# w_up on x before its norm, gains put on by ScalarE, x updated in 1024-wide steps, two more streams begun with pairs of tiles

## The chip, the cores and the metric

One core of a Trainium2 chip. The metric is the device time of one execution in microseconds (us). All times below are us from the start of the profiled span unless marked otherwise.

## The reference, cut to what matters

A state-space and attention block of two layers, then a second block (RWKV and latent attention, a feed-forward net with a causal convolution, and a gated embedding), for 256 tokens of width 2048. All of it is float32. The change lies in the last part of the second block:

```python
h = h + rms_norm_2(mix, post_mix_norm)          # mix = (...) @ w_out
u = rms_norm_2(h, pre_ffn_norm)
up = causal_dwconv(u @ w_up, conv_w, conv_b)    # per channel, over 3 tokens
gate, val = jnp.split(up, 2, axis=-1)
f = (jax.nn.gelu(gate, approximate=True) * val) @ w_down
h = h + rms_norm_2(f, post_ffn_norm)
e = p @ w_ple
h = h + rms_norm_2(jax.nn.sigmoid(h @ w_ple_gate) * e, ple_norm)
```

where `rms_norm_2(x, g) = x * rsqrt(mean(x * x) + 1e-6) * g`, the mean over the 2048 channels of a token. The token's factor is one number per token, so it can be put on before or after the product with w_up.

## The kernel before

Activations lie transposed: x is 16 tiles (k) of 128 channels (partitions) by 256 tokens, side by side in one region, 4096 columns wide. A norm's factor is a number per column (token), held in RS as a 128x256 tile; a gain is a number per partition. So the mean over channels is a sum over tiles (VectorE or TensorE) and over partitions (a TensorE product with ones).

**Products.** Each weight matrix is a *stream* of output tiles n, each the sum over k of blocks of 128x128 weights with 128x256 activations. Both operands are split into a rounded high part (`hi`, a ScalarE copy) and a low part (`lo`, VectorE: value minus high part), and a block is three matmuls of 256 columns: high x high, high x low, low x high. The third waits for the weight's low part. Weights come by DMA in units of 1 MB (16 blocks) into a ring of three places; a unit is split in two *halves* of 8 blocks (1024 columns). A half p has one ScalarE `hi` and one VectorE `lo`, in one of four buffers: `hi` p waits until TensorE has done half p-4. For the activations the same pair of instructions is run for each k (256 wide).

**Order.** One Python class, `Timeline`, plays the schedule once and writes a list of beats; each engine's program goes through this list and emits its part of each beat, so the order on every engine is that of the list, and ScalarE and VectorE wait in order. `stream` (L428) emits, at the start of half p, `hi` of half p+3 and `lo` of half p+2, then the matmuls, and after every half one phase of each tile that is finished but not yet evicted (`leave`, L400; `follow`). The number of phases per kind of tile is in `PHASES` (L238); which phase frees the accumulator bank is in `BANK_FREE`. At a stream's end all phases left over are run at once (`while self.pend: self.follow()`). Streams named in `PAIRS` (L276) begin with their first two tiles interleaved: k 0 to 7 of tile 0, k 0 to 7 of tile 1, k 8 to 15 of tile 0, k 8 to 15 of tile 1. `late` is work put in after block 39 of a stream, with the finished tiles held until then; w_in2 uses both.

**The streams here.** w_out2 (16 tiles of 16 blocks, kind "mo"), w_up (44 tiles), w_down0 (16 tiles of 22 blocks), w_up (44 tiles more), w_ple (16 tiles of 2 blocks), w_down1 (16 of 22), w_pg (16 of 16).
- Eviction of "mo": ScalarE copies 0.5 x the sum to MO, squares it, VectorE adds the square to RS2. Those of "d1" (w_down1) and "pg" (w_pg) end in the same square and addition.
- `rms` (L992, L1325): TensorE product with ones, ScalarE square root; `recip`: VectorE reciprocal into RS.
- `post` (L2049), 16 times: VectorE scales a tile by gain and RS, then adds it to x. It is run after w_out2, after w_down1 and after w_pg (where SyncE writes out every fourth).
- After w_out2: sixteen ScalarE squares of x (`sq`), 16 TensorE products with ones in their wake, a second root and reciprocal; then `h` (L1728) for each k: VectorE product of x, gain and RS, ScalarE high part, VectorE low part. Only then w_up begins. After w_down1, high and low parts of x (`part "xs"`) are made k by k.
- Eviction of w_up, alternately "up0" (gate) and "up1" (value), a pair j makes one hidden tile: ScalarE multiplies the accumulator by the third tap and adds the bias, VectorE adds the two other taps reading the accumulator (255 and 254 columns); up0 goes on with a polynomial (VectorE, three instructions), tanh (ScalarE), a product (VectorE); up1 multiplies by it, and the hidden tile's high part (ScalarE) and low part (VectorE) follow. The phases are one half apart.

L822 is tensor_tensor, L832 scalar_tensor_tensor, L840 reciprocal, L859 activation, L862 matmul: helpers through which every such instruction is recorded.

## Time and profile before

| | us |
|---|---|
| median of three runs (lowest, highest) | 3351.78 (3350.07, 3360.97) |
| the profiled execution | 3350.08 |
| its span | 3348.3 |
| TensorE busy | 3019.5 (90%) |
| VectorE busy | 2286.7 (68%) |
| ScalarE busy | 1623.7 (48%) |
| GpSimd busy | 316.1 (9%) |
| the chain that ended last: TensorE, VectorE, ScalarE, DMA | 63%, 23%, 6%, 5% |

PE is TensorE, PEld its weight loads, DVE VectorE, ACT ScalarE, POOL GpSimd. PEclk is the granted TensorE clock as a share of full speed (2.4 GHz at 1.0, 1.2 GHz at 0.5). A row of a timeline gives the start, the time from the first start to the last end of xN like instructions in a row, and in brackets the idle time before them with what ended it.

### The profile page before, as it was taken

The page shows a single profiled execution, that of the slowest core. Times are in us where ns is not written, and L with a number is a line of the kernel's source. Part 1 is how long each engine was busy: PE and PEld are TensorE (multiplying, and loading weights), DVE is VectorE, ACT ScalarE, POOL GpSimd, SP SyncE. Part 2 cuts the span into 40 slices and gives each one's busy share as a digit, 9 for nine tenths or more (in the row PEclk, how much of TensorE's full clock was granted, in tenths as well). Part 3 has the DMA queues.
Part 4 walks back from the last instruction along what each step waited for, and adds up shares of the span by engine and source line. Part 5 has one row for each costly group of instructions (what it writes and reads, how often), then busy time and mean ns, then how long its engine had stood idle before and what let it go on. Part 6 is the DMA issues. An engine that isn't in the chain of part 4 may idle for free.

```text
span 3348.3 us, 59688 instructions
## 1 busy us (share of the span) xinstructions
PE 3019.5 (90%) x24116; PEld 2777.9 (83%) x24116; DVE 2286.7 (68%) x3591; ACT 1623.7 (48%) x2408; POOL 316.1 (9%) x566
## 2 busy tenths in 40 slices
PE   6799898889998998999899898799899999999977
PEld 1577777768888888998878788789799999999977
DVE  6467776677688867775666666666688745886565
ACT  3345554345465644744444442544455544555443
POOL 0012222100122220200000001010000000000000
PEclk8899999889999998999999998899899999999988
DMA  9776656665644454454323222345355555554533
GB/s 386 282 241 214 221 209 235 239 227 179 166 141 133 148 165 160 167 190 145 107 94 106 96 104 84 135 140 195 114 169 187 183 184 181 184 188 168 181 132 114
DMA packets 110707, 576.92 MB, mean 172 GB/s; under 512 B 33056, under 2 KB 33088, under 8 KB 46688
## 3 DMA queue, kind: packets, MB, share of 16 engines
q1 hardware_dynamic: 89040, 525.37, 45.0%
q0 software_dynamic: 20816, 44.27, 4.6%
q8 instruction: 190, 3.11, 0.4%
q10 hardware_dynamic: 576, 3.47, 0.3%
q14 instruction: 85, 0.70, 0.1%
HBM read 546.83 MB, written 17.83 MB: 169 GB/s over the span
## 4 chain that ended last, share of the span: by engine, by line
PE 63%; DVE 23%; ACT 6%; DMA 5%; issue 3%; SPq 1%; POOL 1%; DVEq 0%; ACTq 0%; POOLq 0%
PE acc L862 62%; DVE arena L822 6%; DVE rounded L822 5%; DVE arena L832 3%; DVE upper L822 3%; DMA arena<-in_w_ada 2%; ACT arena L859 2%; ACT rounded L859 2%; DMA arena<-in_w_in 1%; DVE upper L832 1%; ACT upper L859 1%; DVE upper L840 1%; PE acc L865 1%; SPq L818 1%; ACT L859 1%
## 5 line engine op out<-in xcount | busy, mean ns | idle before, releaser
L862 PE MATMUL acc<-rounded 128*128 128x256 f32 x14832 | 1962.2, 292 | 64.9 <-issue 47.2
L862 PEld LDWEIGHTS acc<-rounded 128*128 128x128 f32 x14832 | 1867.3, 196 | 152.2 <-issue 117.6
L822 DVE TENSOR_TENSOR rounded<-arena,rounded 128x1024 fp32r<-128x1024 f32 (+1 forms) x860 | 1013.7, 1179 | 377.8 <-ACT rounded L859 310.2
L859 ACT ACTIVATE rounded<-arena 128x1024 fp32r<-128x1024 f32 (+1 forms) x876 | 884.4, 1010 | 654.7 <-PE acc L862 501.4
L862 PEld LDWEIGHTS acc<-upper_rounded,rounded 128*128 128x128 f32 x4416 | 546.2, 197 | 40.7 <-DVE rounded L822 21.5
L862 PE MATMUL acc<-upper_rounded,rounded 128*128 128x256 f32 x4416 | 553.6, 288 | 19.3 <-DVE rounded L822 19.2
L862 PE MATMUL acc<-arena 128*32 128x512 f32 (+7 forms) x1898 | 276.0, 465 | 98.3 <-DMA arena<-in_w_ada 43.8
L859 ACT ACTIVATE arena<-arena 128x256 f32<-128x256 f32 (+3 forms) x377 | 191.3, 507 | 237.5 <-DVE arena L822 153.7
L822 DVE TENSOR_TENSOR arena<-arena 128x256 f32<-128x256 f32 (+5 forms) x543 | 264.1, 486 | 40.5 <-ACT arena L859 17.1
L862 PEld LDWEIGHTS acc<-arena 128*32 128x32 f32 (+4 forms) x1898 | 127.2, 141 | 166.8 <-DMA arena<-in_w_ada 65.9
L859 ACT ACTIVATE arena<-acc 128x256 f32<-128x256 f32 (+4 forms) x300 | 125.1, 417 | 254.1 <-PE acc L862 237.1
L862 PE MATMUL acc<-upper 128*128 128x128 f32 (+9 forms) x1632 | 195.1, 298 | 14.8 <-DVE upper L822 10.2
L859 ACT ACTIVATE arena<-acc,arena 128x256 f32<-128x256 f32 (+1 forms) x210 | 100.8, 480 | 183.2 <-PE acc L862 175.7
L862 PEld LDWEIGHTS acc<-upper 128*128 128x128 f32 (+4 forms) x1632 | 155.0, 168 | 40.3 <-DVE upper L822 13.3
L822 DVE TENSOR_TENSOR arena<-acc,arena 128x256 f32<-128x256 f32 (+2 forms) x192 | 81.6, 425 | 152.7 <-PE acc L862 141.8
L832 DVE SCALAR_TENSOR_TENSOR arena<-acc,arena 128x255 f32<-128x255 f32 (+2 forms) x244 | 118.6, 486 | 84.7 <-ACT arena L859 40.2
L832 DVE SCALAR_TENSOR_TENSOR arena<-arena 128x256 f32<-128x256 f32 (+5 forms) x349 | 151.4, 434 | 32.5 <-ACT arena L859 14.1
L818 POOL DMA_DIRECT2D arena<-arena x256 | 130.5, 517 | 423.4 <-ACT arena L859 416.7
L859 ACT ACTIVATE upper<-acc 128x256 f32<-128x256 f32 (+4 forms) x176 | 88.2, 501 | 159.6 <-PE acc L862 112.4
L862 PE MATMUL acc<-upper,arena 64*64 64x64 f32 (+3 forms) x546 | 89.4, 364 | 42.8 <-DVE upper L822 26.4
L862 PEld LDWEIGHTS acc<-upper,arena 128*128 128x128 f32 (+2 forms) x546 | 57.4, 174 | 60.8 <-DVE upper L822 29.8
L865 PE MATMUL acc<-arena 128*128 128x128 f32 x384 | 72.1, 282 | 28.3 <-ACT arena L859 23.0
(88 smaller groups left out, 1170.7 us busy)
## 6 DMA issues: line engine op xcount, KB each, us to landing
arena<-in_w_in SPq DMA_DIRECT2D x164, 1024.0 KB, 5.0
arena<-in_w_ada SPq DMA_DIRECT2D x88, 1024.0 KB, 5.4
arena<-in_w_up SPq DMA_DIRECT2D x88, 1024.0 KB, 4.8
arena<-in_w_down SPq DMA_DIRECT2D x44, 1024.0 KB, 4.9
arena<-in_w_outa SPq DMA_DIRECT2D x16, 1024.0 KB, 7.0
arena<-in_w_glu SPq DMA_DIRECT2D x16, 1024.0 KB, 5.3
arena<-in_w_outm SPq DMA_DIRECT2D x16, 1024.0 KB, 5.0
arena<-in_w_out SPq DMA_DIRECT2D x16, 1024.0 KB, 4.8
```

What stands on the lines that cost most here:

```text
L818: self.e.dma_start(out, in_).then_inc(self.signals.sems[sem], 16)
L822: return self.put(self.e and self.e.tensor_tensor(o, a, b, op))
L832: return self.put(self.e and self.e.scalar_tensor_tensor(out=o, in0=a, scalar=s, in1=b, op0=o1, op1=o2))
L840: return self.put(self.e and self.e.reciprocal(o, a))
L859: return self.put(self.e and self.e.activation(o, a, f, scale=scale, **kw))
L862: return self.put(self.e and self.e.matmul(o, l, r, start=start, stop=stop, skip_group_check=True))
L865: return self.put(self.e and self.e.transpose(o, i, self.m.con("ident")))
```

## The change

- `post` handles four tiles at once: VectorE multiplies 4x256 by RS (repeated), then adds 1024 columns to x. The gains are put on by ScalarE: for w_out2 in the eviction copy (scale 0.5 x post_mix, made once in w_in2's time), for w_down1 and w_pg by an extra copy in place after the square.
- "mo" is squared from the accumulator, ahead of its copy.
- After w_out2 and its reciprocal, `post` of a group alternates with `hf` (high part by ScalarE with the gain as scale, low part by scalar_tensor_tensor on VectorE) and `sqf` (ScalarE squares 1024 columns, GpSimd adds them up). w_up thus runs on x times gain, without the token factor. Its root and reciprocal are `late` in w_up (after block 39), and each w_up tile gets a first phase in which VectorE multiplies the accumulator by RS into a scratch slot; the other phases read that slot.
- After w_down1, high and low parts of x are made 1024 wide (`xs`), each after its `post`.
- w_up and w_pg are in `PAIRS`; `ready` asks for their first units ahead of `recip`.
- `stream` lets held tiles go one at a time.

```diff
-"mo": 3, "up0": 3, "up1": 4
+"mo": 2, "up0": 4, "up1": 5          # PHASES; BANK_FREE of up0, up1: "ev_dve" -> "ev_rs"
...
-PAIRS = (("w_in", 48), ("w_in2", 0))
+PAIRS = (("w_in", 48), ("w_in2", 0), ("w_up", 0), ("w_pg", 0))
...
-            if late is None or blk == 39:
-                if late is not None:
-                    late()
-                    late = None
-                for t in held:
-                    g = self.leave(t)
-                    next(g)
-                    self.pend.append((t, g))
-                held = []
+            if late is not None and blk == 39:
+                late()
+                late = None
+            if held and late is None and (k == nk - 1 or blk % 8 == 7):
+                t = held.pop(0)
+                g = self.leave(t)
+                next(g)
+                self.pend.append((t, g))
...
         self.rms("mo", ("w_out2", 0, 15))
+        self.ready("w_up", 0)
         self.add("recip", "mo")
-        for k in range(16):
-            self.add("post", "mo", k)
-        for k in range(16):
-            self.add("sq", "hf", k)
-        self.rms("hf", None)
-        self.add("recip", "hf")
-        for k in range(16):
-            self.add("h", 3, k)
+        for g in range(5):
+            if g < 4:
+                self.add("post", "mo", g)
+            if g:
+                for k in range(4 * g - 4, 4 * g):
+                    self.add("hf", k)
+                self.add("sqf", g - 1)
         self.add("ff_first")
-        self.stream("w_up", 0, 0, 0, 44, 16)
+
+        def late():
+            self.add("rmsf")
+            self.add("recip", "hf")
+
+        self.stream("w_up", 0, 0, 0, 44, 16, late=late)
...
         self.rms("fo", ("w_down1", 0, 15))
+        self.ready("w_pg", 0)
         self.add("recip", "fo")
-        for k in range(16):
-            self.add("post", "fo", k)
-        for k in range(16):
-            self.add("part", "xs", k)
+        for g in range(5):
+            if g < 4:
+                self.add("post", "fo", g)
+            if g:
+                self.add("xs", g - 1)
...
+    def rmsf():                                    # TensorE
+        pe.wait_ge("sum_pool", ("hf", 3))
+        for i in range(4):
+            x = pe.mm(B(3, 0, 256), con("ones"), V(AR + 256 * i, 256), i == 0, i == 3)
+        x.then_inc("norm_pe", "hf")
...
+    def hf(k):                                     # ScalarE
+        act.wait_ge("x_dve", ("mo", k // 4))
+        act.wait_ge("mm", ("out", tl.out_of["w_out2", 0, 15].o))
+        act.act(m.HT(k)[0], V(X + 256 * k, 256), ACT.Copy, scale=par("pre_ffn", k)).then_inc("h_act", ("f", k))
+
+    def sqf(g):
+        act.act(V(AR + 1024 * g, 1024), V(X + 1024 * g, 1024), ACT.Square).then_inc("norm_act", ("sqf", g))
+
+    def xs(g):
+        act.wait_ge("x_dve", ("fo", g))
+        act.wait_ge("mm", ("out", tl.out_of["w_ple", 0, 15].o))
+        act.act(m.HT4(g)[0], V(X + 1024 * g, 1024), ACT.Copy).then_inc("part_act", ("xs", g))
...
+        elif t.kind == "mo" and ph == 0:
+            act.act(V(tile_ready(act, t.slots[0]), 256), pv, ACT.Square, scale=0.5).then_inc("sq_act", key)
+            act.wait_ge("rw_dve", "init")
+            act.act(V(MO + 256 * n, 256), pv, ACT.Copy, scale=V(GP + n, 1)).then_inc("ev_act", key)
...
         elif t.kind == "d1" and ph == 1:
             square(t, FO + 256 * n, "ev_dve")
+            act.act(V(FO + 256 * n, 256), V(FO + 256 * n, 256), ACT.Copy, scale=par("post_ffn", n)).then_inc("g_act", key)
         elif t.kind == "pg" and ph == 2:
             square(t, EM + 256 * n, "em_dve")
+            act.act(V(EM + 256 * n, 256), V(EM + 256 * n, 256), ACT.Copy, scale=par("ple_norm", n)).then_inc("g_act", key)
...
+    def hf(k):                                     # VectorE
+        hi, lo = m.HT(k)
+        dve.wait_ge("h_act", ("f", k))
+        dve.stt(lo, V(X + 256 * k, 256), par("pre_ffn", k), hi.bitcast(F32), MUL, SUB).then_inc("rhs", ("hf", k))
...
+        dve.ts(V(GP, 16), V(PAR + PCOL["post_mix"], 16), 0.5, None, MUL)
...
-    def post(tag, k):
-        src, g = {"mo": (MO, "post_mix"), "fo": (FO, "post_ffn"), "em": (EM, "ple_norm")}[tag]
-        dve.stt(V(src + 256 * k, 256), V(src + 256 * k, 256), par(g, k), V(RS, 256), MUL, MUL)
-        dve.tt(V(X + 256 * k, 256), V(X + 256 * k, 256), V(src + 256 * k, 256), ADD).then_inc("x_dve", (tag, k))
+    def post(tag, g):
+        src, stream, sem = {"mo": (MO, "w_out2", "ev_act"), "fo": (FO, "w_down1", "g_act"), "em": (EM, "w_pg", "g_act")}[tag]
+        t, x = V(src + 1024 * g, 4, 256), V(X + 1024 * g, 1024)
+        dve.wait_ge(sem, ("ev", tl.out_of[stream, 0, 4 * g + 3].o))
+        dve.tt(t, t, V(RS, (0, 4), (1, 256)), MUL)
+        dve.tt(x, x, V(src + 1024 * g, 1024), ADD).then_inc("x_dve", (tag, g))
...
-        if t.kind in ("rw", "kpe", "cq", "gate") and ph == 0:
+        if t.kind in ("rw", "kpe", "cq", "gate", "up0", "up1") and ph == 0:
             np_ = 32 if t.kind == "rw" and n == 26 else 128
             at = tile_ready(dve, t.slots[0])
             dve.wait_ge("mm", ("out", t.o))
-            dve.tt(V(at, 256, np_=np_), B(b, 0, 256, np_=np_), V(RSH, 256, np_=np_), MUL).then_inc("ev_rs", key)
+            dve.tt(V(at, 256, np_=np_), B(b, 0, 256, np_=np_), V(RS if t.name == "w_up" else RSH, 256, np_=np_),
+                   MUL).then_inc("ev_rs", key)
...
-            dve.stt(V(o + 1, 255), B(b, 0, 255), V(w + 88, 1), V(o + 1, 255), MUL, ADD)
-            dve.stt(V(o + 2, 254), B(b, 0, 254), V(w, 1), V(o + 2, 254), MUL, ADD).then_inc("ev_dve", key)
+            at = TMP + 256 * t.slots[0][0]
+            dve.stt(V(o + 1, 255), V(at, 255), V(w + 88, 1), V(o + 1, 255), MUL, ADD)
+            dve.stt(V(o + 2, 254), V(at, 254), V(w, 1), V(o + 2, 254), MUL, ADD).then_inc("ev_dve", key)
...
+    def sqf(g):                                    # GpSimd
+        pool.wait_ge("norm_act", ("sqf", g))
+        if g:
+            if g > 1:
+                pool.wait_ge("sum_pool", ("hf", g - 1))
+            pool.tt(V(AR, 1024), V(AR, 1024), V(AR + 1024 * g, 1024), ADD).then_inc("sum_pool", ("hf", g))
```

## Rows read from the trace of the kernel before

**Rows 1.** The page: busy us and share of the span, instructions, per engine.

```profile
PE 3019.5 (90%) x24116; PEld 2777.9 (83%) x24116; DVE 2286.7 (68%) x3591; ACT 1623.7 (48%) x2408; POOL 316.1 (9%) x566
```

**Rows 2.** Stretches (us), length, busy us per engine, PEclk, DMA share, GB/s.

```profile
2500.00:2600.00 100.00, 100.00 (x836) 100.00 (x835) 80.22 (x123) 54.61 (x69) 0.00 (x0) 1.00 0.55 188
...
3200.00:3300.00 100.00, 79.30 (x635) 77.80 (x634) 65.75 (x101) 49.31 (x70) 0.00 (x0) 0.90 0.40 137
```

**Rows 3.** Timeline of VectorE, w_out2's end to w_up: start, us, instruction [idle before].

```profile
2396.16 1.75 DVE L840 RECIPROCAL arena<-arena 128x256 f32<-128x256 f32 x1 [1.42 <-ACT arena L859]
2397.95 0.48 DVE L832 SCALAR_TENSOR_TENSOR arena<-arena 128x256 f32<-128x256 f32 x1
...
2413.16 0.42 DVE L822 TENSOR_TENSOR arena<-arena 128x256 f32<-128x256 f32 x1
2415.42 1.75 DVE L840 RECIPROCAL arena<-arena 128x256 f32<-128x256 f32 x1 [1.84 <-ACT arena L859]
```

**Rows 4.** Timeline of ScalarE, the same stretch and w_up's third tile.

```profile
2393.36 0.38 ACT L859 ACTIVATE arena<-acc 128x256 f32<-128x256 f32 x1 [1.76 <-PE acc L862]
...
2394.36 1.28 ACT L859 ACT_TABLE_LOAD   x1
...
2447.52 0.57 ACT L859 ACTIVATE arena<-acc,arena 128x256 f32<-128x256 f32 x1 [1.26 <-PE acc L862]
```

**Rows 5.** Stretches: one us after w_pg's first matmul at 3228.76.

```profile
3231.00:3232.00 1.00, 1.00 (x7) 1.00 (x6) 0.79 (x3) 0.00 (x0) 0.00 (x0) 0.51 0.00 0
```

**Rows 6.** VectorE by form: instruction, shapes, count, busy us, mean ns, idle before.

```profile
L822 DVE TENSOR_TENSOR arena<-acc,arena 128x256 f32<-128x256 f32 x143 | 60.7, 424 | 99.9 <-PE acc L862 91.8
...
L822 DVE TENSOR_TENSOR upper<-upper,arena 128x1024 f32<-128x1024 f32 x16 | 19.6, 1226 | 1.1
...
L832 DVE SCALAR_TENSOR_TENSOR rounded<-arena,rounded 128x256 fp32r<-128x256 f32 x16 | 8.2, 513 | 2.3 <-ACT rounded L859 0.8
```

**Rows 7.** ScalarE by form, whole span.

```profile
L859 ACT ACTIVATE rounded<-arena 128x1024 fp32r<-128x1024 f32 x802 | 852.0, 1062 | 630.6 <-PE acc L862 501.4 <-DMA arena<-in_w_in 59.7 <-DMA arena<-in_w_outa 17.6
...
L859 ACT ACTIVATE rounded<-upper,arena 128x256 fp32r<-128x256 f32 x32 | 16.3, 508 | 26.4 <-DVE upper L832 25.9
```

**Rows 8.** Timeline of GpSimd while x's last squares are summed.

```profile
1358.92 1.44 POOL L822 TENSOR_TENSOR arena<-arena 128x256 f32<-128x256 f32 x2 [1.53 <-ACT arena L859]
```

**Rows 9.** Timeline of VectorE, the same stretch and just before.

```profile
1349.78 1.22 DVE L822 TENSOR_TENSOR rounded<-arena,rounded 128x1024 fp32r<-128x1024 f32 x1
...
1359.76 1.69 DVE L822 TENSOR_TENSOR rounded<-arena,rounded 128x1024 fp32r<-128x1024 f32 x1
```

**Rows 10.** Timeline of VectorE in steady w_up.

```profile
2563.32 1.00 DVE L832 SCALAR_TENSOR_TENSOR arena<-acc,arena 128x255 f32<-128x255 f32 x2 [0.58 <-ACT arena L859]
...
2565.66 1.22 DVE L822 TENSOR_TENSOR rounded<-arena,rounded 128x1024 fp32r<-128x1024 f32 x1
...
2569.08 1.00 DVE L832 SCALAR_TENSOR_TENSOR arena<-acc,arena 128x255 f32<-128x255 f32 x2 [0.32 <-ACT arena L859]
...
2572.50 1.22 DVE L822 TENSOR_TENSOR rounded<-arena,rounded 128x1024 fp32r<-128x1024 f32 x1 [0.63 <-ACT rounded L859]
...
2574.84 1.00 DVE L832 SCALAR_TENSOR_TENSOR arena<-acc,arena 128x255 f32<-128x255 f32 x2 [0.58 <-ACT arena L859]
```

**Rows 11.** Timelines at w_up's two ends, VectorE, then TensorE.

```profile
2684.28 1.00 DVE L832 SCALAR_TENSOR_TENSOR arena<-acc,arena 128x255 f32<-128x255 f32 x2 [1.64 <-ACT arena L859]
...
2686.75 5.22 DVE L822 TENSOR_TENSOR rounded<-arena,rounded 128x1024 fp32r<-128x1024 f32 x4
...
3067.78 13.34 PE L862 MATMUL acc<-rounded 128*128 128x256 f32 x96 [3.98 <-issue]
```

**Rows 12.** Timelines at w_pg's start, VectorE, then ScalarE.

```profile
3207.87 0.42 DVE L822 TENSOR_TENSOR arena<-arena,acc 128x256 f32<-128x256 f32 x1 [3.44 <-PE acc L862]
...
3243.80 0.48 ACT L859 ACTIVATE arena<-acc,arena 128x256 f32<-128x256 f32 x1 [1.14 <-PE acc L862]
```

**Rows 13.** Timeline of VectorE, the last instruction.

```profile
3344.78 0.42 DVE L822 TENSOR_TENSOR arena<-arena 128x256 f32<-128x256 f32 x1
```

More of the change, by code:

```diff
@@ L745, in run @@
         self.add("recip", "em")
-        for k in range(16):
-            self.add("post", "em", k)
+        for g in range(4):
+            self.add("post", "em", g)
         self.add("end")
@@ L900, in moving @@
     if name == "w_up":
-        return m.HT(k), ("h", 3, k)
+        return m.HT(k), ("hf", k)
+    if name == "w_pg":
+        return m.HT(k), ("xs", k // 4)
     if name in ("w_down0", "w_down1"):
         return m.FP(k), ("ft", k + 22 * (name == "w_down1"))
-    tag = {"q_up": "cq", "w_bmla": "ya", "w_out2": "mx", "w_ple": "p", "w_pg": "xs"}[name]
+    tag = {"q_up": "cq", "w_bmla": "ya", "w_out2": "mx", "w_ple": "p"}[name]
     return m.HT(k), (tag, k)
@@ L1358, in part @@
         free = {"yr": ("w_in2", 0, 67), "ya": ("w_brw", 0, 15), "mx": ("w_bmla", 0, 15), "p": ("w_up", 0, 87),
-                "xs": ("w_ple", 0, 15), "cq": ("w_in2", 0, 67)}
+                "cq": ("w_in2", 0, 67)}
         if isinstance(tag, str):
@@ L1533, in ev @@
         pv = B(b, 0, 256)
-        if ph == 0 and t.kind not in ("xa", "xo", "xf", "rw", "kpe", "cq", "gate", "brw", "bmla", "d1"):
+        if ph == 0 and t.kind not in ("xa", "xo", "xf", "rw", "kpe", "cq", "gate", "brw", "bmla", "up0", "up1", "d1"):
             act.wait_ge("mm", ("out", t.o))
@@ L2146, in ev @@
                 dve.stt(f, V(FT + 512, 256), 0.5, V(o, 256), MUL, MUL).then_inc("f_dve", ("f", j))
[L2147 removed]
+        elif t.kind == "up0" and ph == 3:
             q = V(FT + 512, 256)
@@ L2150, in ev @@
             dve.stt(q, q, 1.0, V(FT, 256), ADD, MUL).then_inc("f_dve", ("g", n // 2))
-        elif t.kind == "up1" and ph == 3:
+        elif t.kind == "up1" and ph == 4:
             j = n // 2
@@ L2368, in s5_u8, with post @@
             sp.dma(V(U8 + 1024 * half, 32, 32, p0=16 * q, np_=16), src, f"s5_u8{half}", (l, q))
-    def post(tag, k):
-        if tag == "em" and k % 4 == 3:
-            sp.wait_ge("x_dve", (tag, k))
-            sp.dma(out[:, k - 3:k + 1], V(X + 256 * (k - 3), 4, 256), "out", k)
+    def post(tag, g):
+        if tag == "em":
+            sp.wait_ge("x_dve", (tag, g))
+            sp.dma(out[:, 4 * g:4 * g + 4], V(X + 1024 * g, 4, 256), "out", g)
     play = dict(fetch=fetch, s5_u8=s5_u8, post=post)
@@ L2378, in sync_program @@
             play[beat](*of)
-    sp.wait_ge("out", 15)
+    sp.wait_ge("out", 3)
 def build_program(nc, D, out):
```

83 lines of the change are left out of this document (34 added, 49 removed).

## The prediction

> **What bounds the kernel now.** I read the page's shares first: TensorE is busy 90% of the span, VectorE 68%, ScalarE 48% [rows 1]. A share is a mean, so next came the table of stretches. In the feed-forward part TensorE is busy all the time at full clock, with VectorE at 80% [rows 2]; there, nothing that shortens another engine's work gains anything. The stretch with w_down1's end is at 79% and clock 0.90 [rows 2]: there TensorE waits, and the timelines show the same at w_out2's end and at the kernel's end. Three places are left to gain from: the two norms that stand between streams, and the tail.
>
> **Place A, w_out2 to w_up.** The last tile's eviction starts at 2393.36 [rows 4]. VectorE then runs the reciprocal (1.75), sixteen pairs "scale, add to x" at 0.98 a pair (2397.95 to 2413.58), a second reciprocal at 2415.42 and sixteen products with their low parts [rows 3]. The third w_up tile is evicted at 2447.52, by a ScalarE that waited for TensorE [rows 4]. A tile takes 5.76 (half the 11.52 from 2563.32 to 2574.84, where TensorE is the limit [rows 10]; 48 matmuls of 0.12, so 0.36 a block and 2.88 a half of 8 blocks). Three tiles back from 2447.52 is 2430.24, the start that a w_up at full pace would have had. The gap costs 36.9.
>
> After the change the square and the scaled copy of the last tile swap places on ScalarE and the table load still follows them, so the reciprocal still ends near 2397.9; the low part of half 504, now ahead of it, fits in the wait. Then on VectorE:
> - additions to x: eight 1024-wide instructions, 1.23 each [rows 6] plus 0.03, 10.1 in all, where there were 15.7;
> - sixteen low parts as scalar_tensor_tensor, 0.51 [rows 6] plus 0.06: 9.1. The sum of squares, the second root and reciprocal and sixteen products have left this chain. ScalarE's part (four copies with a per-partition operand, 0.51 [rows 7], and one 1024-wide square, some 1.15, per group: 3.4) stays beside VectorE's 4.8 per group.
> So x is ready at 2417.1, and half 505's low part, queued behind it, at 2418.4.
> TensorE starts at about 2403.6 with what is there. A restart runs at half clock: 0.50 to almost 3232, 3.2 after the restart of 3228.76 [rows 5]. With the tiles in pairs, the first 16 of 32 blocks need only k 0 to 7 of x; the third eight follow k 8 to 15 as they come, and the last eight need half 505's low part for every third matmul. They end 8 x 0.36 less two matmuls after it: about 2421.2. That is two tiles, so the equivalent start is 2409.7.
>
> **The GpSimd additions.** The squares are added by GpSimd in three 1024-wide instructions amid this chain. The trace has its nearest case where x's final squares are summed: two 256-wide additions take 1.44 [rows 8], and VectorE's 1024-wide low part that starts during the second takes 1.69, where without GpSimd it takes 1.22 [rows 9]. So 0.46 was lost, about what was left of GpSimd's instruction. Four times 0.72 is 2.9 for a 1024-wide one; I take 2.6 of block each (0.46 of 0.72 would give 1.9; bounds 0 and 2.9). They come after group 1, group 2 and group 3, each while VectorE has work: 7.8, moving 2421.2 to 2429 and the equivalent start to 2417.4.
> The Trainium skill (SBUF — State Buffer, Who interferes with whom) says that a Vector instruction with two SBUF inputs contends with a GpSimd one that reads SBUF and that the later one blocks fully. The trace agrees at 256 wide (1.69 beside 1.22); no row shows 1024 wide. A sum that left the rule out would be 7.8 shorter, which is rival 1.
>
> **The norm moved into w_up.** TensorE now does four fp32 matmuls of 256 columns amid the stream, about 1.8 (before, the squares' matmuls lay in its idle time). VectorE waits for the root behind them (4 or so after its low parts of halves 506 to 508), then has a reciprocal of 1.75 and the evictions of three tiles held back. Walking its queue against TensorE's halves, two low parts (halves 513 and 514) come 0.6 and 1.0 late: 1.8 with the rounding. Equivalent start 2417.4 + 3.6 = 2421.1; bound of the lag from below 0, from above 8, if each of three evictions costs a pair's 2.4. **A gains 9.1** (16.9 without GpSimd's block).
>
> **Every w_up tile.** One instruction is added, PSUM times RS, 0.42 [rows 6] plus 0.04 to 0.11 of hand-over. VectorE's period for two tiles is 11.52, of which it waits for ScalarE 0.58, 0.63 and 0.32 [rows 10], 1.53. Its work is 9.99 and becomes 10.9 to 11.1: under 11.52. These waits end with ScalarE work that doesn't depend on how late VectorE is; they are slack and can be used up. At the fullest point (odd tile's end: low part of the hidden tile, taps and polynomial of the even tile 2.34 (2563.32 to 2565.66 [rows 10]), product, weight low part) the weights are ready 4.8 after TensorE enters the half, and it needs them after 5.75. Cost zero; cover 0.5 per pair. If it is gone, the bound is two added instructions, 1.0 per pair, x44 = 43.
>
> **Ends of w_up.** The phases left over are run at the end before the next weights. Before, the end of the first w_up has VectorE's last conv at 2684.28 (eviction waited for 1.64), and the next low parts from 2686.75 [rows 11]. Now the taps and polynomial of the last even tile (2.34, before done a half earlier), a product and one more hand-over between engines lie behind the last matmul: hidden low part ready 6.9 after it instead of 3.1. First end: the weight low part comes 8.2 after, needed after 6.0: **2.2 lost**, where TensorE had not waited. Second end: TensorE already waits 3.98 for w_ple's input [rows 11]; the whole shift is added: **3.7 lost**. Bounds for both 3 to 8.
>
> **Place B, w_down1 to w_pg.** From 3207.87, the last addition, to 3243.80, the second tile's eviction [rows 12], less 11.52: start 3232.3. After: the copy with post_ffn puts the table load, and all behind, 0.5 later; reciprocal to 3213.0. VectorE: eight additions 10.1, four 1024-wide low parts at 1.33, 5.3 (ScalarE's 1.06 copies [rows 7] lie beside), the last ready at 3228.5. TensorE, at half clock to about 3226.5, is behind this: four blocks 3219.4 to 3222.3, four 3223.4 to 3226.3, then 24 at 0.36, end 3235.0, start 3223.6. **B gains 8.7**; bounds 7 and 10.
>
> **Tail.** The last addition ends at 3345.20 [rows 13]. Sixteen pairs of 0.98 (15.7) become eight of 1.26 (10.1), less 0.5 for the scaled copy before the table load: **5.0**; bounds 4.5 and 5.6.
> In w_in2 a small product comes in (0.2) and one eviction leaves a wait (0.45): counted as nothing.
>
> **Sum.** 9.1 - 2.2 - 3.7 + 8.7 + 5.0 = 16.9. The profiled execution took 3350.08 (span 3348.3), 1.7 under the median of the three runs, 3351.78. So 3333.2 by the one and 3334.9 by the other; I say 3334.
>
> **Rivals.**
> 1. GpSimd does not block, since its additions are short or fall between: 3334 - 7.8 = 3326. For it: its spans are rough in the trace. Against: 1.69 beside 1.22. Chance 0.20.
> 2. The start of w_up lags longer. With 0.5 of slack a pair, VectorE makes up little, and each stall by its recip and the held tiles reaches TensorE: 8 instead of 1.8, and the ends of w_up cost 8 instead of 5.9: 3342. For it: the like late norm in w_in2 has VectorE almost without pause. Chance 0.17.
> 3. VectorE becomes the bound of w_up, **slower than before**. Place: the 44 pairs. It decides once the added 0.98 finds less than 0.6 of the 1.53 of waits to fill (16.9 / 44 = 0.38 more per pair than 11.52 eats the gain). If none is filled: 3334 + 43 = 3377; if half of the added 0.98 is hidden, 3355. For it: the phases alternate VectorE, ScalarE, VectorE, and the order is fixed. Against: the hand-overs are half a tile (2.88) apart. Chance 0.08.
> 4. The change doesn't do what it says: w_up's first matmul still waits for all of x. Then the 32 blocks follow the last low part, 2425 + 11.5 and 1.6 for the clock, 2438 in place of 2429: 9 later, 3343. The waits are by k, which speaks against it. Chance 0.03.
> The forecast itself has 0.52.
>
> **The numbers.** 0.3% is 10 us, about what a measurement tells here from no change: faster means under 3341.7. Forecast, rival 1 and some of rival 2 and 4 lie under it: 0.80. Within: most of rival 2 and 4, 0.13. Slower: 0.07. The range takes in rival 1 with B and the tail at their better bounds, and rival 2: 3320 to 3347.
>
> **What would show it.** The reciprocal after w_out2 still near 2398; then eight 1.23 instructions on VectorE, three of them or their neighbours stretched by 2 or more beside GpSimd; the first w_up matmul near 2403.6 and half clock to past 2411; VectorE in w_up at about 88% busy with TensorE at 100%; TensorE idle about 2 at w_down0's start and 7.7 before w_ple; w_pg's first matmul 6 to 7 after the reciprocal's end; 13 to 14 from the last reciprocal to the end. The forecast is wrong if TensorE is under 99% inside w_up, or no VectorE instruction is stretched.

## The result, and the profile after

The changed kernel takes 3323.6 us (median of five runs, 3318.3 to 3325.1) where the kernel before took 3350.1 in the same session (five, 3342.9 to 3361.0): ratio 0.9917, 95% interval 0.9895 to 0.9939. It was timed twice more as a measure for experiments, on two chips, with 0.9921 (0.9906 to 0.9937) and 0.9917 (0.9902 to 0.9932). The forecast was 3334, range 3320 to 3347, faster with 0.80. The sign and the range held. The gain is 26 to 28 us by the three ratios, though, where the sum had 16.9, and that asks for an account.

The profiled execution took 3322.7 (span 3320.9). I cut both traces at four instructions that exist in both: the start of the reciprocal after w_out2, w_down0's first matmul, the reciprocal after w_down1, and the last reciprocal.

| stretch | before | after | gained | predicted |
|---|---|---|---|---|
| ahead of the first reciprocal | 2396.16 | 2391.61 | 4.55 | 0 |
| to w_down0's first matmul (place A, first w_up) | 287.32 | 277.71 | 9.6 | 9.1 |
| to w_down1's reciprocal (w_down0, second w_up, w_ple) | 527.23 | 529.29 | -2.1 | -6.4 (2.2, 3.7, and 0.5 for the copy of w_down1's last tile) |
| to the last reciprocal (place B, w_pg) | 117.07 | 107.12 | 9.9 | 8.7 |
| to the end (tail) | 20.52 | 15.17 | 5.35 | 5.6 (its copy, -0.5, lies in the row above, which has w_down1's 0.5 back) |

The prediction's 2.2 at w_up's first end stands in the third row: it was to be a wait 6 us into w_down0, behind the cut.

The page's shares answer to [rows 1]: TensorE's busy time fell by 12, and VectorE's rose by 22 (88 products of 0.42, less what the norm and the additions gave up).

```profile
PE 3007.5 (91%) x24092; PEld 2772.4 (83%) x24092; DVE 2308.3 (70%) x3580; ACT 1640.0 (49%) x2416; POOL 323.9 (10%) x569
```

**Place A.** The timeline of VectorE answers to [rows 3]; the columns are start, duration, instruction, count and idle time before.

```profile
2391.61 1.75 DVE L850 RECIPROCAL arena<-arena 128x256 f32<-128x256 f32 x1 [0.59 <-ACT arena L869]
2393.47 5.07 DVE L832 TENSOR_TENSOR arena<-arena 128x1024 f32<-128x1024 f32 x4
2398.66 2.27 DVE L842 SCALAR_TENSOR_TENSOR rounded<-arena,rounded 128x256 fp32r<-128x256 f32 x4
...
2403.62 6.05 DVE L842 SCALAR_TENSOR_TENSOR rounded<-arena,rounded 128x256 fp32r<-128x256 f32 x4
...
2412.37 6.59 DVE L842 SCALAR_TENSOR_TENSOR rounded<-arena,rounded 128x256 fp32r<-128x256 f32 x8
...
2428.39 1.75 DVE L850 RECIPROCAL arena<-arena 128x256 f32<-128x256 f32 x1 [4.11 <-ACT arena L869]
```

The eight additions are there at 1.23. Four low parts take 2.27 where nothing disturbs them; the second four took 6.05 and the last eight 6.59 instead of 4.6. GpSimd's timeline of the same stretch says why:

```profile
2402.86 2.86 POOL L832 TENSOR_TENSOR arena<-arena 128x1024 f32<-128x1024 f32 x1 [120.25 <-ACT arena L869]
2406.94 2.45 POOL L832 TENSOR_TENSOR arena<-arena 128x1024 f32<-128x1024 f32 x1 [1.22 <-ACT arena L869]
2415.70 2.39 POOL L832 TENSOR_TENSOR arena<-arena 128x1024 f32<-128x1024 f32 x1 [6.30 <-ACT arena L869]
```

Each addition stands over a stretched group: 3.8 and 2.0 lost, 5.8 in all (7.8 predicted). It is one low part for each addition: those that start at 2403.62, 2407.28 and 2415.90, while GpSimd is at work, take 2.38, 2.39 and 2.47 instead of 0.48, and each ends 0.3 after GpSimd's instruction. From the reciprocal's end to the last low part it is 25.6, where the sum had 27.0. TensorE's timeline shows what reaches it:

```profile
2399.25 2.90 PE L872 MATMUL acc<-rounded 128*128 128x256 f32 x12 [8.80 <-issue]
2406.05 2.29 PE L872 MATMUL acc<-rounded 128*128 128x256 f32 x9 [3.91 <-DVE rounded L842]
2409.73 7.76 PE L872 MATMUL acc<-rounded 128*128 128x256 f32 x45 [1.38 <-DVE rounded L842]
2418.42 1.44 PE L872 MATMUL acc<-rounded 128*128 128x256 f32 x8 [0.93 <-DVE rounded L842]
2420.34 5.78 PE L872 MATMUL acc<-rounded 128*128 128x256 f32 x46 [0.48 <-DVE rounded L832]
2425.96 1.89 PE L872 MATMUL acc<-arena 128*128 128x256 f32 x8
2427.50 17.85 PE L872 MATMUL acc<-rounded 128*128 128x256 f32 x146
2445.77 1.10 PE L872 MATMUL acc<-rounded 128*128 128x256 f32 x7 [0.43 <-DVE rounded L832]
```

The four fp32 matmuls of the sum are at 2425.96, about 1.5 of them on the path; one more stall of 1.36 follows at 2450.27, so the lag behind the late norm is 0.43 + 1.36 = 1.8, the size that the sum gave it.

**Inside w_up.** One pair of tiles on VectorE in the first w_up (answers to [rows 10]):

```profile
2560.57 1.47 DVE L842 SCALAR_TENSOR_TENSOR arena<-arena 128x255 f32<-128x255 f32 x3
2562.14 0.42 DVE L832 TENSOR_TENSOR arena<-acc,arena 128x256 f32<-128x256 f32 x1
2562.67 2.55 DVE L832 TENSOR_TENSOR rounded<-arena,rounded 128x1024 fp32r<-128x1024 f32 x2
2565.33 0.42 DVE L832 TENSOR_TENSOR upper_rounded<-arena,upper_rounded 128x256 fp32r<-128x256 f32 x1
2565.86 1.00 DVE L842 SCALAR_TENSOR_TENSOR arena<-arena 128x255 f32<-128x255 f32 x2
...
2568.22 0.42 DVE L832 TENSOR_TENSOR arena<-acc,arena 128x256 f32<-128x256 f32 x1
...
2571.94 1.47 DVE L842 SCALAR_TENSOR_TENSOR arena<-arena 128x255 f32<-128x255 f32 x3
```

and a stretch of 100 us from there, answering to [rows 2]:

```profile
2560.00:2660.00 100.00, 100.00 (x836) 100.00 (x835) 88.89 (x143) 55.42 (x71) 0.00 (x0) 1.00 0.55 189
```

TensorE is at 100% and VectorE at 89%, as said. But no bracket is left on VectorE: its pair takes 11.37 without a single wait, against TensorE's 11.52. The cover is 0.15, not 0.5. Eighty-nine per cent busy was full.

This is VectorE working off what the late norm left it behind, 0.15 a pair, and it goes on like this to the end of the first w_up. In the second w_up it keeps TensorE's pace, a pair every 11.52, with one wait in each:

```profile
2905.90 0.42 DVE L832 TENSOR_TENSOR arena<-acc,arena 128x256 f32<-128x256 f32 x1 [0.26 <-PE acc L872]
...
2917.42 0.42 DVE L832 TENSOR_TENSOR arena<-acc,arena 128x256 f32<-128x256 f32 x1 [0.26 <-PE acc L872]
```

The bracket says 0.26, and the pair is 0.15 longer than without it. So some 0.1 of a bracket is not slack.

**The ends of w_up.** After the first, TensorE goes into w_down0 and on without a wait (2.2 predicted); the second (answers to [rows 11]) went from 3.98 to 4.52, 0.5 for the 3.7 predicted:

```profile
3054.38 7.85 PE L872 MATMUL acc<-rounded 128*128 128x256 f32 x44 [4.52 <-issue]
```

From 3054 to 3060 the granted clock is 0.52 in the mean. It was at half from 3052.88 to 3059.71, 5.3 of it behind the wait; in the kernel before it was at half for 3.4 behind the wait. That is 1.0 lost, and with the 0.5 of wait and 0.5 for the copy it makes the row's 2.1.

**Place B and the tail** (answers to [rows 12, 13]), VectorE first:

```profile
3195.22 0.42 DVE L832 TENSOR_TENSOR arena<-arena,acc 128x256 f32<-128x256 f32 x1 [3.39 <-PE acc L872]
...
3198.61 1.75 DVE L850 RECIPROCAL arena<-arena 128x256 f32<-128x256 f32 x1 [0.63 <-ACT arena L869]
3200.46 5.07 DVE L832 TENSOR_TENSOR arena<-arena 128x1024 f32<-128x1024 f32 x4
...
3305.73 1.75 DVE L850 RECIPROCAL arena<-arena 128x256 f32<-128x256 f32 x1 [1.96 <-ACT arena L869]
3307.59 10.25 DVE L832 TENSOR_TENSOR arena<-arena 128x1024 f32<-128x1024 f32 x8
```

```profile
3206.96 2.90 PE L872 MATMUL acc<-rounded 128*128 128x256 f32 x12 [9.56 <-issue]
3210.83 27.97 PE L872 MATMUL acc<-rounded 128*128 128x256 f32 x231 [0.97 <-DVE rounded L832]
```

w_pg's first matmul comes 6.6 after the reciprocal's end (6 to 7 said), and eight additions of 1.23 end the kernel.

### The profile page after: what moved, and what is told of

Same layout as the page of the kernel before. It is cut to its first block, busy times and chain, and to the rows that moved or that the text cites. A ratio compares the mean times of both kernels' runs of the same rounds, so it can differ in the third digit from the quotient of the medians.

```text
span 3320.9 us, 59768 instructions
## 1 busy us (share of the span) xinstructions
PE 3007.5 (91%) x24092; PEld 2772.4 (83%) x24092; DVE 2308.3 (70%) x3580; ACT 1640.0 (49%) x2416; POOL 323.9 (10%) x569
## 4 chain that ended last, share of the span: by engine, by line
PE 63%; DVE 23%; ACT 6%; DMA 4%; issue 3%; POOL 1%; SPq 0%; DVEq 0%; ACTq 0%; POOLq 0%
PE acc L872 62%; DVE arena L832 7%; DVE rounded L832 5%; DVE upper L832 2%; ACT arena L869 2%; DVE arena L842 2%; ACT rounded L869 2%; DMA arena<-in_w_ada 2%; DMA arena<-in_w_in 1%; DVE upper L842 1%; ACT upper L869 1%; DVE upper L850 1%; PE acc L875 1%; DVE rounded L842 1%; DVE arena L838 1%
## 5 line engine op out<-in xcount | busy, mean ns | idle before, releaser
L869 ACT ACTIVATE arena<-arena 128x256 f32<-128x256 f32 (+4 forms) x469 | 248.9, 531 | 302.6 <-DVE arena L832 210.9
L832 DVE TENSOR_TENSOR arena<-arena 128x256 f32<-128x256 f32 (+6 forms) x519 | 273.2, 526 | 52.0 <-ACT arena L869 30.3
L842 DVE SCALAR_TENSOR_TENSOR arena<-arena 128x256 f32<-128x256 f32 (+5 forms) x461 | 205.7, 446 | 42.7 <-ACT arena L869 14.5
L832 DVE TENSOR_TENSOR arena<-acc,arena 128x256 f32<-128x256 f32 (+3 forms) x280 | 119.1, 425 | 162.3 <-PE acc L872 144.3
L872 PEld LDWEIGHTS acc<-upper 128*128 128x128 f32 (+4 forms) x1632 | 155.3, 169 | 35.0 <-issue 12.8
L869 ACT ACTIVATE arena<-acc,arena 128x256 f32<-128x256 f32 (+1 forms) x154 | 66.3, 430 | 100.7 <-PE acc L872 92.8
```

Source lines behind the costliest of these rows:

```text
L832: return self.put(self.e and self.e.tensor_tensor(o, a, b, op))
L842: return self.put(self.e and self.e.scalar_tensor_tensor(out=o, in0=a, scalar=s, in1=b, op0=o1, op1=o2))
L869: return self.put(self.e and self.e.activation(o, a, f, scale=scale, **kw))
L872: return self.put(self.e and self.e.matmul(o, l, r, start=start, stop=stop, skip_group_check=True))
```

## The experiments

All numbers marked "chain" are from the start of the reciprocal after w_out2 to the end of the span: 952.1 before, 929.3 changed. Ahead of that reciprocal every engine has the same instructions in the same order in the changed kernel and the experiments (but for the copy of numbers 6 and 10), and yet it starts between 2385.1 and 2397.1 in their profiles. The chain leaves that out; times of single runs do not. I cut the chain as in the table above: A, M (to w_down1's reciprocal), B, tail.

### 1. No pairs

```diff
-PAIRS = (("w_in", 48), ("w_in2", 0), ("w_up", 0), ("w_pg", 0))
+PAIRS = (("w_in", 48), ("w_in2", 0))
-        self.ready("w_up", 0)      # and ("w_pg", 0)
+        self.split_ahead(self.halves + NS - 1)
```

> The changed kernel without the pairs: w_up and w_pg run tile 0 whole, then tile 1 (the weights asked for early as before). If the pairs fill TensorE's wait for the later k (theory): in the changed kernel 32 w_up blocks were done about 29.8 us after the reciprocal's end; now the first tile ends with the last low part and 16 more blocks follow at 0.36, so 2 us later; the same 2 us in w_pg. Together 4 us longer from w_out2's last eviction to the end (932.1 in the changed kernel). Rival, the pairs do nothing, since the low parts of the weights, queued behind those of x, come last anyway: within 1 us of 932.1.

One run, 3322.3 us, with its reciprocal 6.3 earlier than in the changed kernel's profile. Chain 935.2: A 281.0 (+3.3), B 109.6 (+2.5). The time alone would have said that pairs are worth nothing; the chain says 5.8 (4 expected). In A two more waits of TensorE appear, 2.17 and 1.29 where it had 0.93 and 0.48, and the clock stays at 0.50 for thirty microseconds after the reciprocal instead of 23.

### 2. GpSimd's additions behind the low parts

```diff
     def sqf(g):
+        pool.wait_ge("rhs", ("hf", 15))
         pool.wait_ge("norm_act", ("sqf", g))
```

> The changed kernel with GpSimd's three 1024-wide additions held back until VectorE has made the last low part of x for w_up. Theory, a GpSimd addition blocks VectorE: the three bursts of scalar_tensor_tensor after the reciprocal take 0.57 an instruction (2.27 for four; they took 6.05 for four and 6.59 for eight), the last low part is ready 19.8 us after the reciprocal's end where it was 25.6, and the 1024-wide low parts of the weights right behind are stretched instead, by some 6 in all. Rival, the stretch was ScalarE's or a wait of VectorE's on data: the bursts stay as long as they were.

3317.4 us; chain 928.8, A 275.3 (-2.4), B 109.5 (its clock came back late, below). VectorE and then GpSimd:

```profile
2398.77 2.25 DVE L842 SCALAR_TENSOR_TENSOR rounded<-arena,rounded 128x256 fp32r<-128x256 f32 x4
...
2403.72 4.61 DVE L842 SCALAR_TENSOR_TENSOR rounded<-arena,rounded 128x256 fp32r<-128x256 f32 x8
2408.43 11.19 DVE L832 TENSOR_TENSOR rounded<-arena,rounded 128x1024 fp32r<-128x1024 f32 x4
```

```profile
2408.47 10.07 POOL L832 TENSOR_TENSOR arena<-arena 128x1024 f32<-128x1024 f32 x3 [130.76 <-DVE rounded L842]
```

With the additions gone from beside them, the second four low parts take 2.25 (6.05 before) and the last eight 4.61 (6.59): the block was 5.8 and was GpSimd's doing. It moved behind: four low parts of weights, 5.2 when alone, take 11.19 beside three additions. That is the Trainium skill's rule again (SBUF — State Buffer, Who interferes with whom), and the trace agrees at 1024 wide too: the two engines take turns. The first low part (1.23) is under way when the first addition starts, and the addition ends 2.26 after it; the next low part, begun meanwhile, ends 1.08 after the addition; the next addition 2.26 after that; and so on to the end. TensorE then waits 2.64 for the sum, so that 2.4 of the 5.8 reach A.

### 3 and 4. How much room VectorE has in w_up

Number 3 makes the product with RS twice for every tile; number 4 adds one product of 64 columns for every second tile.

```diff
+            if t.name == "w_up":                  # 3
+                dve.tt(V(at, 256), B(b, 0, 256), V(RS, 256), MUL)
+            if t.kind == "up1":                   # 4
+                dve.tt(V(at, 64), B(b, 0, 64), V(RS, 64), MUL)
```

> The changed kernel with each w_up tile's product with RS done twice (88 more VectorE instructions of 0.42, in w_up alone). By the changed kernel's trace VectorE repeats every 11.37 us for a pair of tiles without a pause, against TensorE's 11.52: 0.15 of slack. Then two more of 0.46 to 0.53 make 12.3 to 12.4, and 44 pairs cost 35 to 40 us, and TensorE falls under 95% in w_up. By the prediction's sum (work of 10.9 to 11.1 a pair): 12.0, 18 to 24 us. If VectorE's lag is hidden by the ring of weights: under 5 us.

> The changed kernel with one more small VectorE product (64 columns, about 0.22 and its hand-over, 0.26 to 0.33) per pair of w_up tiles. With a slack of 0.15 a pair: 11.63 to 11.70 against 11.52, so 0.11 to 0.18 x 44 = 5 to 8 us longer in w_up. With the prediction's slack of 0.4 to 0.6 a pair: nothing, under 1 us.

One run of each. Number 3: 3366.5 us, slower than the kernel before (3350.4 on that chip); from the first reciprocal to w_down1's, A and M together, 845.7 instead of 807.0, 38.7 more. Number 4: 3338.7 us; 817.5, 10.5 more. TensorE in number 3:

```profile
2560.76 11.77 PE L872 MATMUL acc<-rounded 128*128 128x256 f32 x96 [0.52 <-DVE rounded L832]
2573.04 11.77 PE L872 MATMUL acc<-rounded 128*128 128x256 f32 x96 [0.52 <-DVE rounded L832]
```

The period of a pair is now 12.28 = 11.37 + 2 x 0.455: every added instruction comes through whole, once 0.15 is used up. In number 4 VectorE's pair takes 11.62 (2571.02 to 2582.64), 0.10 over TensorE's. Its 10.5, more than the 5 to 8 expected, come in three places. Inside the first w_up, where VectorE starts late from the norm, 3.3 (A is 281.0). In w_down0 a wait of 2.89 and half clock behind it, some 1.3:

```profile
2687.15 18.13 PE L872 MATMUL acc<-upper_rounded,rounded 128*128 128x256 f32 x138 [2.89 <-DVE rounded L832]
```

And ahead of w_ple a wait of 7.28 instead of 4.52, 2.8; the second w_up itself loses nothing on TensorE. So VectorE was 0.15 per pair from being the bound, rival 3 of the prediction. It also shows what the ends cost when VectorE runs late through a whole stream.

### 5. The squares summed by TensorE

```diff
-        self.stream("w_up", 0, 0, 0, 44, 16, late=late)
+        self.stream("w_up", 0, 0, 0, 44, 16, late=late, sums={3: 0, 7: 1, 19: 2, 23: 3})
+    def sqp(g):                 # takes the place of GpSimd's sqf and of rmsf's matmuls
+        pe.wait_ge("norm_act", ("sqf", g))
+        for k in range(4 * g, 4 * g + 4):
+            x = pe.mm(B(3, 0, 256), con("ones"), V(AR + 256 * k, 256), k == 0, k == 15)
```

> The changed kernel, with the squares of x summed by TensorE: sixteen fp32 matmuls against the ones, four at a time, behind w_up's blocks 3, 7, 19 and 23 where TensorE waits for low parts anyway; GpSimd's three additions and the four late matmuls go. My theory (GpSimd's block costs 5.8 on VectorE's chain, the late matmuls 1.5 on TensorE, the stalls behind the second reciprocal 1.8): from the first reciprocal's start to w_down0's first matmul 270 to 272 us instead of 277.7, the sixteen low parts of x done 20 after the reciprocal's end instead of 25.6; the time 6 to 8 below the changed kernel, 3315 to 3318. Rival: the chain is not what sets w_up's start, TensorE at half clock is; then sixteen matmuls of about 0.45 come to its path, 7 us, for 1.9 removed, and the kernel is as fast as the changed one or up to 2 us slower, 3323 to 3326.

> The kernel with the squares summed by TensorE once more, beside the changed kernel on the same chip. Its profile was 6.5 us shorter than the changed kernel's from the first reciprocal of the feed-forward part to the end (922.8 against 929.3), but its times were not (ratio to before 0.9933, the changed kernel's 0.9917 and 0.9921). If the profile is right and the times met by chance a slow draw of the part ahead of that reciprocal, which differs by 12 us among profiles of equal code, this run gives a ratio of 0.989 to 0.991, 3314 to 3319 us. If the times are right and something ahead of the feed-forward part is slower with this program, it stays at 0.993 and its first reciprocal lies later than the 2387.7 of its first profile, at 2393 or more.

> The changed kernel, unaltered, as the measure for the run beside it: ratio 0.990 to 0.994. In the profile the chain from the first reciprocal of the feed-forward part to the end takes 929.3, or 2.4 more if TensorE's clock comes back late in w_pg.

In both profiles A is 271.4 (271.37 and 271.35; changed kernel 277.71, 277.71 and 277.72 in its three), 6.3 less, as expected. The sixteen matmuls fill waits, and TensorE no longer stops between 2395.3 and 2439.7:

```profile
2395.30 2.90 PE L874 MATMUL acc<-rounded 128*128 128x256 f32 x12 [8.80 <-issue]
2398.00 3.21 PE L874 MATMUL acc<-arena 128*128 128x256 f32 x8
2400.86 1.78 PE L874 MATMUL acc<-rounded 128*128 128x256 f32 x12
...
2413.21 26.49 PE L874 MATMUL acc<-rounded 128*128 128x256 f32 x218
```

Its clock is back at 1.00 some 13 us after the reciprocal's start instead of 23. The times don't follow: ratio 0.9933 (0.9918 to 0.9949), then 0.9915 (0.9901 to 0.9929) beside the changed kernel's 0.9917 on the same chip, 3319.5 and 3320.2 us. Six microseconds are 0.0018; each ratio has 0.0015 or so to either side, and the difference of two has about 0.002, so the runs can neither show nor exclude them. The chain is 922.8 and 925.1 (the second with a late clock in w_pg), against 929.3. The second profile's reciprocal lay at 2391.57, between the two cases that I had set apart. Whether the gain is lost ahead of that reciprocal in most executions or hidden by their scatter stays open.

### 6. The last tile's scaled copy behind the square root

On top of number 5, for the last tile of w_out2, w_down1 and w_pg.

```diff
     def rms(tag, total):
         act.wait_ge("norm_pe", tag)
         act.act(V(RS, 256), B(3, 0, 256), ACT.Sqrt, ...).then_inc("norm_act", ("sqrt", tag))
+        if tag in last:
+            gain(tag, last[tag])
```

> The previous kernel, and ScalarE makes the last tile's scaled copy behind the square root, where the changed kernel makes it before the root's table load (w_out2, w_down1, w_pg). My theory: table load, root and reciprocal all come 0.4 to 0.5 us earlier three times, and the copy fits beside the reciprocal of 1.75, since only the fourth group's addition needs it: 1.2 to 1.5 us below the previous kernel, so 3314 to 3317, 7 to 9 below the changed kernel. Rival: the square's matmul and not the table load comes last before the root, so nothing changes against the previous kernel.

3312.2 us, ratio 0.9899 (0.9884 to 0.9915). The wait ahead of w_up falls from 8.80 to 8.31 and that ahead of w_pg from 9.56 to 9.04, so the theory held where it can be read: 0.5 each. The time is 8 below number 5's in the same session, of which this explains 1.5; the rest no part of the chain shows.

### 7. The changed kernel with w_up on normalized x

Squares, second root, reciprocal and sixteen products stand ahead of w_up again; wide steps, ScalarE's copies and pairs stay.

```diff
-        for g in range(5):  ... post, hf, sqf
+        for g in range(4):
+            self.add("post", "mo", g)
+        for k in range(16):
+            self.add("sq", "hf", k)
+        self.rms("hf", None)
+        self.add("recip", "hf")
+        for k in range(16):
+            self.add("h", 3, k)
```

> The changed kernel with w_up on the normalized x, as before the change: squares of each 256 columns on ScalarE, summed by TensorE, second root and reciprocal, then sixteen products with their low parts; no product in the evictions. The 1024-wide additions, the scaled copies on ScalarE and the pairs stay. This sizes the one part from which the change takes its name. My theory: before, w_up's start in equal pace lay 32.3 after the first reciprocal's end (2397.95 to 2430.24); the wide additions take 5.6 from it and the pairs 3, which gives 24; in the changed kernel it lies 22.5 after it, stalls included, and its last tile's phases cost 0.5 more before w_ple. So the moved norm is worth 1 us here: this kernel at 3323 to 3326. Rival: the moved norm carries the gain, because it takes the root and sixteen products out of the chain (the prediction's sum without GpSimd's block has it at 8): this kernel at 3330 or more.

3324.8 us, ratio 0.9935 (0.9919 to 0.9952). Chain 932.3: A 280.1 (2.4 more than changed), M 527.5 (1.8 less), B 109.5 (2.35 more). In B the two kernels issue the same instructions. What differs is the clock (granted share, third column from the end), first this kernel, then the changed one:

```profile
3211.74:3214.74 3.00, 2.25 (x11) 1.96 (x10) 2.86 (x3) 1.06 (x1) 0.00 (x0) 0.50 0.00 0
3214.74:3217.74 3.00, 2.77 (x13) 2.77 (x14) 2.76 (x4) 0.21 (x1) 0.00 (x0) 0.50 0.02 5
3217.74:3220.74 3.00, 3.00 (x17) 3.00 (x17) 2.79 (x3) 1.91 (x2) 0.00 (x0) 0.58 0.00 0
```

```profile
3207.61:3210.61 3.00, 2.25 (x11) 1.96 (x10) 2.86 (x3) 1.06 (x1) 0.00 (x0) 0.62 0.00 0
3210.61:3213.61 3.00, 2.78 (x23) 2.78 (x24) 2.76 (x4) 0.21 (x1) 0.00 (x0) 1.00 0.01 3
```

Without that difference, the moved norm is worth 2.4 - 1.8 = 0.6 us: as built, the part that names the change does almost nothing for the time. With its squares summed by TensorE (number 5) it is worth 7 by the chain: GpSimd's block is most of what eats it.

### 8. The wide steps alone

Number 7's kernel without pairs (its edit and number 1's).

> One part of the change alone: the 1024-wide additions and low parts of x and the scaled copies on ScalarE; w_up runs on normalized x and neither w_up nor w_pg begins with pairs. My theory: the wide steps carry the larger part of the gain. Eight 1024-wide instructions for sixteen pairs give 5.6 less 0.5 for the copy in each of three places, 15, and the pairs were worth 5.8 in profiles: between the kernel before and the changed one, 6 over the changed kernel's time, ratio to before 0.993 to 0.995. Rival: without the norm moved and without pairs the first place gains little, since sixteen products and low parts still follow the second reciprocal: ratio 0.996 or more.

3333.5 us (nine runs), ratio 0.9958 (0.9946 to 0.9971): the expected 0.993 to 0.995 is missed on the small side. Chain 938.0: A 283.6, M 527.5, B 111.8, tail 15.2. Against before that is 14.1 gained (3.7, -0.2, 5.3, 5.3), 0.0042, as the ratio has it. In B its clock came back 12.8 us after the restart (0.50 in 3225 to 3227, 0.69 in the next two), where the kernel before had it back after about 3.3 [rows 5]; with equal clocks the wide steps are worth 16.4. I had put 5.1 into A. It gave 3.7: after a wide addition ScalarE has four squares to make and not one, and VectorE waits 3.46 for the second root in number 7's profile, whose A has the same order there, and 1.84 in [rows 3].

### 9. The changed kernel once more

> The changed kernel once more, on this chip, as the measure for the other two: the same 3319 to 3326 us and ratio 0.990 to 0.994 as before. In the profile the chain from the first reciprocal of the feed-forward part to the end should repeat within 1 us for w_up (277.7) and take 107.1 or 109.5 for w_pg, by when TensorE's clock comes back; what lies before that reciprocal may differ by 5 us or more, since nine profiles with the same code before it had it from 2385 to 2397.

3321.8 us, ratio 0.9921. Chain 929.3, its four pieces within 0.05 of the first profile's, with the first reciprocal 2.2 earlier. Chains repeat to a tenth; what is ahead of them doesn't.

### 10. w_ple behind w_down1

On top of number 6. w_ple's 32 blocks need only p; they now run while VectorE makes the norm of w_down1's result.

```diff
-        self.stream("w_ple", 0, 0, 0, 16, 2)
-        self.stream("w_down1", 0, 22, 0, 16, 22)
-        self.rms("fo", ("w_down1", 0, 15))  ... recip, post, xs
+        self.stream("w_down1", 0, 22, 0, 16, 22, sums={39: [("part", "p", 0), ("part", "p", 1)]})
+        self.stream("w_ple", 0, 0, 0, 16, 2, sums={
+            4: [("rms", "fo", ("w_down1", 0, 15)), ("recip", "fo"), ("post", "fo", 0)],
+            10: [("post", "fo", 1), ("xs", 0)], 18: [("post", "fo", 2), ("xs", 1)],
+            26: [("post", "fo", 3), ("xs", 2)]})
```

> The kernel with the sums on TensorE and the copies behind the roots, and besides w_ple's stream (16 tiles of two blocks, 11.5 us of TensorE, which need nothing but p) stands behind w_down1 instead of ahead of it. Its parts of p go where they meet no one, and the root's matmul, the reciprocal and the additions of w_down1's norm stand amid its blocks. My theory: TensorE's waits of 4.52 ahead of w_ple, 1.5 ahead of the root's matmul and 9.0 ahead of w_pg are filled by work that is there anyway, and its clock stays at full: of 15 us, some 3 to 4 go again for three low parts of w_pg's weights (1.3 each) that now stand in VectorE's chain. So 10 to 12 below the previous kernel, 3301 to 3306. Rival: VectorE's chain from w_down1's last tile to the last low part of x sets the end, and the low parts, which wait for TensorE to leave w_ple's halves, and ScalarE's sixteen evictions between the copies stretch it by 8 or more: 0 to 5 below.

3303.9 us, ratio 0.9871 (0.9854 to 0.9888), the fastest: 45 us under the kernel before on that chip, 18 under the changed one. Chain 910.7, 11.2 below number 6's 921.9: A and M together are 16.4 shorter, and B, which now holds w_ple, is 5.2 longer. TensorE over the place where it stood idle for 9.6:

```profile
3165.53 1.97 PE L870 MATMUL acc<-rounded 128*128 128x256 f32 x15
3167.33 0.59 PE L870 MATMUL acc<-arena 128*128 128x256 f32 x2
3167.57 3.58 PE L870 MATMUL acc<-rounded 128*128 128x256 f32 x27
3171.71 1.69 PE L870 MATMUL acc<-rounded 128*128 128x256 f32 x12 [0.56 <-ACT arena L867]
...
3176.64 2.42 PE L870 MATMUL acc<-rounded 128*128 128x256 f32 x18 [1.84 <-ACT arena L867]
...
3192.15 18.03 PE L870 MATMUL acc<-rounded 128*128 128x256 f32 x147 [0.82 <-DVE rounded L830]
```

```profile
3170.00:3190.00 20.00, 14.77 (x112) 13.50 (x110) 18.14 (x15) 14.48 (x25) 0.00 (x0) 1.00 0.16 54
```

The granted clock stays at 1.00 through the place. The waits that are left are short: for ScalarE, whose evictions of w_ple's tiles stand between the weights' and x's copies, and for VectorE's low parts.

## Why the prediction came out as it did

**Where the gain comes from.** By the chain, at equal clocks in w_pg: wide steps 16.4 (number 8), pairs 5.8 (number 8 to 7: A 3.45, B 2.3; number 1 from the other side: 3.3 and 2.5), the moved norm 0.6 (number 7). Together 22.8, against 16.9 predicted. Of the 6 between them, 4.3 is the ends of w_up, 1.2 place B and 0.5 place A, less 0.3 in the tail. The runs have 4 to 5 more, and so has the first row of the table. It lies ahead of all that the argument was about. The changed kernel and the experiments with the moved norm start the reciprocal at 2390.5 in the mean of nine profiles, the kernels on normalized x at 2395.1 to 2396.2 in three; but numbers 7 and 8 have the changed kernel's order up to there, and single profiles of the nine reach 2397.1. What sets it was not found, and three profiles against nine that scatter by 12 do not show that it belongs to the change. That the range held is in part luck: 3323.6 is 3.6 above its lower bound, and the range reached down so far for rival 1, which number 2 refutes. What took the time there were the ends of w_up, which cost less than said, and the unexplained part ahead of the argument, some 4 us each and both the same way.

**Place A: mechanism right, size of the block off.** The prediction had 9.1 there; measured 9.6. Its step "2.6 of block each, 7.8" measured 5.8. Its steps for the additions (10.1 against 10.2), the low parts (9.1 against 9.2 undisturbed), the sum's matmuls (1.8 against 1.5) and the lag (1.8) stand. With 2.0 less of block it should have been 11.1; TensorE's waits and half clock up to 2414.6, against "past 2411", are the likely place of the 1.5 between, which no run took apart.

**"Ends of w_up" failed.** The prediction put 2.2 and 3.7 on the path; measured 0 and 0.5, and 1.0 of half clock behind it. It reckoned all phases of the last tiles from TensorE's last matmul. But VectorE's order is a list, and TensorE's position doesn't tie it: the even tile's taps started at 2668.17, 1.1 before TensorE left w_up at 2669.3, because nothing in the list ahead of them waited. Only the odd tile's product, taps and low part really follow the last matmul. The last hidden tile's low part was ready 4.8 and 3.9 after it, where the prediction had 6.9. For the second w_up with w_ple and w_down1 the moved norm cost 1.8 in all (M, number 7 against the changed kernel).

**"Every w_up tile: zero, cover 0.5 per pair" gave the right cost from a wrong margin.** The step took the bracketed waits of [rows 10], 1.53 in all, as slack that could be used up whole. But when an instruction is ready at once, behind one of another engine, some 0.10 still lie between it and the one ahead (2562.04 to 2562.14 above). Those hand-overs were inside the brackets. Work 9.99, two products of 0.42 + 0.11, and three times 0.10 that was never slack: 11.35, measured 11.37. Numbers 3 and 4 bear it out. Rival 3, at 0.08, was nearer than it looked: by the prediction's own 0.38 per pair over 11.52, 0.53 more work per pair would have eaten its sum. Number 4's 0.25 took 10.5 of the gain, number 3's 0.91 took all of it.

**Place B: 8.7 against 9.9.** The instructions came as laid out. The prediction assumed half clock "to about 3226.5", 7 us from w_pg's start; in this profile full clock was back after about 3, in others of equal code after nine. With the late clock B is 109.5 and the gain 7.6. The prediction's value lies between.

**Rival 1** (GpSimd doesn't block, 3326) names a time near the measured one for a reason that number 2 refutes. **Rival 2** had its condition right and its cost wrong: VectorE did run late through all of the first w_up, but TensorE's last wait for it is the 1.36 at 2450.27. **Rival 4** fell: w_up's first matmul came after group 0 of x, 5.9 after the reciprocal's end.

What stays open: the 6 us of number 5 that the profiles show and the runs don't, the 1.5 in place A, and what moves the first reciprocal.

## What to carry to other kernels

Before filling an engine's "waits" with work, see which of them would shrink to nothing: here each hand-over between engines left about a tenth of a microsecond, so an engine at 89% of busy time may have no room at all. Where a reduction stands between two matmul streams, first shorten it with wide instructions, then look for a stream with no stake in it and put that there; it beat everything else tried here. Take a profile apart at instructions that both kernels have before you explain a difference of their times.

## What the runs showed of the hardware

- A 1024-wide GpSimd addition held up the one VectorE instruction with two inputs that started beside it: 2.38 to 2.47 us instead of 0.48. When VectorE had such work all the time, the two took turns, and three additions that took 2.86, 2.45 and 2.39 in the changed kernel took 10.07 (number 2), so the loss is mutual.
- The same code got TensorE's clock back at different times after the same wait (9.56, or 9.04 in number 6): about 3 us after the restart in some profiles, 8 to 9 in others (B 106.6 to 107.2 in six of the ten profiles with this B, 109.1 to 109.6 in four). It is worth 2.4 us and comes with no change of code.
- VectorE's tensor_tensor took 0.225 us for 64 columns (number 4), 0.425 for 256 and 1.226 for 1024: one straight line, by these three some 0.16 fixed and 1.04 ns a column (an estimate from them). From the accumulator and from SBUF 256 columns took the same.
- VectorE left 0.03 to 0.04 us between two instructions of one chain and 0.10 ahead of one that asks for another engine's semaphore, though it was long set.
